# Squared-relu layers of a two-block network: the leftover work of a matrix product is queued ahead of the next weight splits, and the norm's sums one product later

## The reference, cut to what matters

```
def sq_relu_mlp(h, w1, w2):
    u = jax.nn.relu(h @ w1)
    return (u * u) @ w2
...
x = x + sq_relu_mlp(rmsnorm_2(x, norm_mlp[layer]), w_mlp1[layer], w_mlp2[layer])
```

## Time and profile before

| | |
|---|---|
| median of three executions | 2423.24 us (2422.3 to 2423.79) |
| profiled execution: its own time | 2421.31 us |
| profiled execution: span of the program's instructions | 2419.5 us |
| PE busy | 2366.7 us (98%) |
| DVE busy | 1327.2 us (55%) |
| ACT busy | 1064.4 us (44%) |

### The profile page before, as it was taken

The page is one execution under the profiler, slowest core; times in us unless marked ns, Lnnn a source line. Parts: engine busy times, 40 slices in busy tenths (PEclk is TensorE's granted clock), DMA queues, the critical chain, the costliest instruction groups (busy, mean ns, idle before and its releaser), DMA issues.

```text
span 2419.5 us, 30917 instructions
## 1 busy us (share of the span) xinstructions
PE 2366.7 (98%) x12252; PEld 1945.0 (80%) x12252; DVE 1327.2 (55%) x2135; ACT 1064.4 (44%) x1759; POOL 232.8 (10%) x189
## 2 busy tenths in 40 slices
PE   9999999999999999999999999999999999999998
PEld 8888888777777788888887667989987677888987
DVE  5533436788654345433335866735645676753653
ACT  4323224455432334322323456624624785741642
POOL 0100100322102010100100200001000100100100
PEclk9999999999999999999999999999999999999999
DMA  4323223211122131323222215536522112644641
GB/s 153 99 87 104 99 84 102 84 53 53 62 70 73 55 118 62 113 86 106 96 86 88 82 46 133 148 105 157 140 96 64 38 48 67 163 122 123 162 117 69
DMA packets 72864, 230.68 MB, mean 95 GB/s; under 512 B 8080, under 2 KB 16528, under 8 KB 72464
## 3 DMA queue, kind: packets, MB, share of 16 engines
q1 hardware_dynamic: 66384, 206.34, 26.0%
q0 software_dynamic: 6048, 22.02, 5.5%
q10 hardware_dynamic: 288, 0.34, 0.0%
HBM read 226.57 MB, written 2.10 MB: 95 GB/s over the span
## 4 chain that ended last, share of the span: by engine, by line
PE 84%; DVE 6%; ACT 5%; issue 3%; DMA 2%; POOL 0%; POOLq 0%; DVEq 0%; ACTq 0%
PE bank L2158 21%; PE bank L2162 21%; PE bank L2160 21%; PE bank L2176 3%; PE bank L2178 3%; PE bank L2180 3%; PE bank L2342 2%; DMA wraw<-in_stream 2%; ACT whi L2463 2%; PE bank L2304 1%; PE bank L2349 1%; DVE wlo L2807 1%; PE bank L2249 1%; PE bank L2245 1%; PE bank L2247 1%
## 5 line engine op out<-in xcount | busy, mean ns | idle before, releaser
L2807 DVE TENSOR_TENSOR wlo<-wraw,whi 128x1024 fp32r<-128x1024 f32 (+3 forms) x462 | 518.0, 1126 | 552.4 <-ACT whi L2463 551.6
L2463 ACT ACTIVATE whi<-wraw 128x1024 fp32r<-128x1024 f32 (+3 forms) x462 | 435.1, 948 | 470.4 <-PE bank L2162 377.0
L2158 PE MATMUL bank<-hhi,whi 128*128 128x512 f32 x1288 | 514.7, 400 | 2.3 <-ACT hhi L2508 1.0
L2162 PE MATMUL bank<-hhi,wlo 128*128 128x512 f32 x1288 | 504.1, 391 | 1.6 <-DVE wlo L2807 1.5
L2160 PE MATMUL bank<-hlo,whi 128*128 128x512 f32 x1288 | 503.3, 391 | 0.4 <-DVE hlo L2858 0.4
L2158 PEld LDWEIGHTS bank<-hhi,whi 128*128 128x128 f32 x1288 | 242.2, 188 | 56.6 <-issue 6.7
L2162 PEld LDWEIGHTS bank<-hhi,wlo 128*128 128x128 f32 x1288 | 241.7, 188 | 56.0 <-DVE wlo L2807 4.1
L2160 PEld LDWEIGHTS bank<-hlo,whi 128*128 128x128 f32 x1288 | 242.4, 188 | 50.0 <-DVE hlo L2858 2.6
L2160 PE MATMUL bank<-mlo,whi 128*128 128x512 f32 x448 | 176.8, 395 | 0.2 <-DVE mlo L3164 0.2
L2158 PE MATMUL bank<-mhi,whi 128*128 128x512 f32 x448 | 176.9, 395 | 0.0
L2162 PE MATMUL bank<-mhi,wlo 128*128 128x512 f32 x448 | 176.9, 395 | 0.0
(11 more groups left out here) (459 smaller groups left out, 4224.6 us busy)
## 6 DMA issues: line engine op xcount, KB each, us to landing
wraw<-in_stream SPq DMA_DIRECT2D x335, 512.0 KB, 3.4
wraw<-in_stream POOLq DMA_DIRECT2D x34, 512.0 KB, 6.0
wraw<-in_stream SPq DMA_DIRECT2D x32, 192.0 KB, 2.3
wraw<-in_stream SPq DMA_DIRECT2D x22, 256.0 KB, 2.6
rot_tables<-in_stream SPq DMA_DIRECT2D x8, 512.0 KB, 5.5
rot_tables<-in_stream POOLq DMA_DIRECT2D x8, 512.0 KB, 5.5
wraw<-in_stream SPq DMA_DIRECT2D x26, 128.0 KB, 2.0
wraw<-in_stream SPq DMA_DIRECT2D x8, 320.0 KB, 2.9
```

The source lines that it names most:

```text
L2158: pe.matmul(out, sh, xh, start=first, stop=False)
L2162: p = pe.matmul(out, sl, xh, start=False, stop=end and last)
L2463: act.activation(whi[j][:, 0:L], src[:, 0:L], F.Copy).then_inc(*hi.up(c))
L2807: dve.tensor_tensor(wlo[j][:, 0:L], src[:, 0:L], whi[j][:, 0:L].bitcast(f32), SUB).then_inc(*lo.up(c))
```

## The change

```
@@ in multiplied
+                later()
                 at_once, then = product(f, name, (*afree, *open_sums["h", s].tok) if f == 12 else afree)
-                later()
                 if (f, name) == (4, "p5"):
                     put("token_last", s, ("used", CH[(f"m{l}u", 3, 0)]))
                 at_once()
@@ in mlp
-                owed = chain_of([open_sums[R.next].pay_one] * 7, [R.step] * 2)
+                owed = chain_of([open_sums[R.next].pay_one] * 7, [int], [R.step] * 2)
```

## The result

The changed kernel ("after" from here on) takes 2469.15 us as the median of four executions (2467.54 to 2472.26), beside 2423.51 us (2422.3 to 2424.18) for the kernel before: a ratio of 1.0189, with a 95% interval of 1.0177 to 1.0202. It is slower, as forecast, but by about 46 us instead of 31, and the time lies above the end of the range, 2462. The profiled execution of after took 2472.26 us with a span of 2470.5, which is 51.0 more than the span before.

The account below looks back on a forecast made before the run. ACT and DVE, alternating in strict order, would bind blocks instead of TensorE: losses per half 7.7 + 6.4 + 8.6 + 6.4 = 29.1, plus 2.5 half clock, on 2421.31 gives 2452.9; median 1.9 higher, said 2454 us, range 2439 to 2462.

Parts of the forecast that it names:

- every named wait: TensorE waits for c22's sum ahead of q4 in blocks 4, 8, 20, 24, 2.5 to 4 us; root ahead of spread, 4 to 5.
- the ring: Closed loop of ACT and DVE steps through one block: 22.8 us where blocks follow each other, against TensorE's 20.06; chance 0.66.
- no change: Rival: transfers end the splits' waits, so the order behind them is free and 2423 us stay; chance 0.06.
- The forecast's own links: Start-to-start times between ACT and DVE steps in a block, 0.48 to 1.33 us each, summed to the block's time.
- the first half's 24.0: Block time in a layer's first half, with the norm's additions in between at 0.60 us each: 24.0 us.
- Half clock: TensorE at 1.2 GHz after waits, on top of the waits: 0 to 5.2 us, taken as 2.5.
- The root's place: Norm's root behind q7's low part on DVE: spread waits 4.7 us, q2 of block 12 comes 7.7 us late.
- the clock falls often: Rival: five waits of 2.7 to 4.7 us per layer, each with its half clock: about 2461 us; chance 0.08.
- the 31.6 of the forecast: Total predicted loss over both layers: 29.1 us from late products plus 2.5 for half clock.

Follow-up runs that it names:

- the first edit alone: On the kernel before, what is left of a product goes ahead of the next product's splits, the norm's additions staying where they were: 2465.33 us, ratio 1.0175.
- the small sums: Seven eighths of GpSimd's accumulating transfers left out: on the changed kernel 2452.89 us, ratio 1.0119; on the kernel before 2416.71 us, ratio 0.9978.
- the second edit: Run by itself on the kernel before: the norm's sums one product later, the order of corners and splits as it was; 2419.32 us, ratio 0.9985.
- half of the load: The changed kernel with half of the load of q4's chunk left out: 2462.74 us, ratio 1.0165.
- all but c11: On the kernel before, what is left of q7, q4 and q3 goes ahead of the next splits, corner c11 keeping its order: 2440.68 us, ratio 1.0069.
- c21 and c12: On the kernel before, what is left of q4 and q3 goes ahead of the next splits, q2 and q7 keeping their order: 2444.29 us, ratio 1.0095.
- the run with early additions: On the kernel before, the norm's seven additions each one product earlier, its sums and root where they were: 2422.95 us, ratio 0.9994.

## Why the prediction was off, point by point

**The direction and the mechanism were right.** TensorE had almost no idle time to give back, ACT and DVE alternate once `later` stands ahead of the splits, every named wait appeared (ACT's relu waits 1.89 us for the corner sum, its copy 2.62 for c22's min), and the sums no longer wait. The rule of strict order within ACT and DVE that the prediction cited from the Trainium skill, "Perfetto Trace Analysis", section on the Tensor Engine instruction, agrees with these runs: the first edit alone changes nothing but the order within the queues, and costs 2465.33 - 2422.39 = 42.9 us, which it would not if a split could pass a waiting corner.

**The step that failed is the sum of the ring, "Together 22.8 us".** It put q4's split 0.48 us behind the hold and had no transfer in it. But the load of q4's chunk starts when q2's low part is done, and that low part is a link of the same ring; the load took 7.4 to 8.5 us, so q4's split waited 2.0 to 3.1 us in blocks 8, 20 and 24, and a block took 25.05 to 26.18 us. The row was there: ACT waited 1.47 us for a DMA at the splits of q4 and q3. I read it only as an argument for "no change" and not as a further arm of the loop. The forecast's own links would have given it: they put q4's split 15.79 - 10.35 + 1.14 = 6.58 us behind the start of q2's low part, and in place of that stand the 1.23 us of this low part and the load. So a block takes 22.81 - 6.58 + 1.23 = 17.5 us and the load: with the 6.7 us that the load took before 24.2, an estimate from these rows, and with the 8.15 of after 25.6, against 25.78 measured. Inside the layers after stands 48.1 us behind, and 31.0 with the small sums: 17.1 us, of which at least 11 (17.1 less the 6 that the small sums give the kernel before) are this missing term.

**The links themselves were right to 0.4 us.** With the load out of the way the ring is 23.24 instead of 22.8 and 24.19 instead of 24.0. In the second halves most of the 0.4 is an instruction that the sum left out: c12's low part, 0.61 start to start, stands on DVE ahead of q4's low part, which therefore started at 1720.14 and not 1.08 behind its high part, at 1719.81. In the first half's 24.0 it is one of the three 0.60, though the text calls them additions.

**Half clock was mis-sized.** I took 2.5 us. The places are 10 in these layers, about 39 us at 1.2 GHz; most lie under a wait, but behind the spread and behind the last long q4 of each layer they counted 1.6 + 0.8 + 1.4 + 1.6 = 5.4 us against the starts before. One at p6 of block 4 put off the next product by 1.5 us, but not the half: q4 of block 4 waits for c22 anyway and comes 3.5 us late, as in the first edit alone, where p6 ran at full clock. A smaller slip: the forecast's own sum gives 2454.8, and I said 2454.

**The root's place** cost a wait of 3.0 and 3.1 us, not 4.7: TensorE came to the spread later than reckoned, since block 8's q4 ahead of it ran partly at half clock (q3 behind it started 1.5 us later than q4 against before).

**The rivals.** Nearest was "the clock falls often", 2461, for the wrong reason: after lost 48.1 us inside the layers, 16.5 more than the 31.6 of the forecast, and at least 11 of these were the load and 5.4 - 2.5 = 2.9 the clock. That the second edit takes the wait from the sums was right, and by itself it gains a little (0.9985), although 1.0 us of waiting moved to the spread; beside the first edit nothing of it is left.

What stays open: why the load takes 6.2 us in one kernel and 9.0 in another beside the same three transfers of POOL. The traces narrow it down, at blocks 8, 20 and 24 of both layers. Where the corners c21 and c12 go ahead of the splits (after, first edit alone, half of the load, all but c11, c21 and c12), POOL starts its last two transfers 2.5 and 2.0 us ahead of the load, and the load lands 0.15 to 0.69 us behind the last of them. In the other kernels with whole sums POOL starts them 0.9 and 0.3 us ahead of the load, and it lands 1.85 to 3.87 us before the last of them, in 6.2 to 7.6 us. So the change also moved the load against those transfers; no run moved these starts alone.

## What to carry to other kernels

When an order makes two engines wait for each other in turn, sum every closed path, the one through a buffer's reload too: a load that starts when a split has read its place is a link as much as the split is, and a wait on a DMA that costs nothing before the change is the sign of it. Take the load's time from the place where it runs, beside the transfers that it shares the DMA engines with. And a wait that is removed from one step is only gone if what stands ahead of the next step in its queue moves too, as with the root of the norm.

## What was not expected of the hardware

Half of a load was hardly faster than a whole one: 256 KB took 6.6 to 7.7 us and 512 KB 7.4 to 8.5 us beside three accumulating transfers of 512 KB, while 512 KB took 3.4 to 5.0 us when those were cut to 64 KB. And TensorE's clock fell to 1.2 GHz at ten places in the layers of after, nine of them in or behind waits of 3.0 to 4.6 us, but not after every wait: behind the 2.26 us ahead of block 4's q4 the granted clock was 1.00 for 25 us (2.4 GHz), and in the run with early additions the spread waited 1.53 us and the 7 us around it had a granted clock of 1.00, where the wait of 1.50 before gave 0.76.
